# Strassen pairs for the gate and up tiles of the second group's second feed-forward

## The reference

```python
def _swiglu(x, w_gate, w_up, w_down):
    return (jax.nn.silu(x @ w_gate) * (x @ w_up)) @ w_down
x = _layer_norm(ALPHA * x + 0.5 * _swiglu(x, p['ffn2_gate'], p['ffn2_up'], p['ffn2_down']), p['ln4_g'], p['ln4_b'])
```

## Time and profile before

| | us |
|---|---|
| median of 3 runs | 2529.02 (2528.16 to 2529.35) |
| span of the profiled execution | 2523.5 |
| PE busy | 2437.7 (97%) |
| POOL busy | 1376.1 (55%) |
| ACT busy | 982.3 (39%) |
| DVE busy | 920.9 (36%) |
| the stretch from the second feed-forward of group 1 to the end | about 2105 to 2523 |

### The profile page before, as it was taken

The page is one execution under the profiler, slowest core; times in us unless marked ns, Lnnn a source line. Parts: engine busy times, 40 slices in busy tenths (PEclk is TensorE's granted clock), DMA queues, the critical chain, the costliest instruction groups (busy, mean ns, idle before and its releaser), DMA issues.

```text
span 2523.5 us, 39960 instructions
## 1 busy us (share of the span) xinstructions
PE 2437.7 (97%) x16311; PEld 2217.3 (88%) x16311; DVE 920.9 (36%) x1775; ACT 982.3 (39%) x1736; POOL 1376.1 (55%) x860
## 2 busy tenths in 40 slices
PE   8999999999999999998999999999899999999998
PEld 8888889888999999987789877888659899999998
DVE  1000002266810004277452689997264333000003
ACT  4333333534333233455543533333473435333231
POOL 4776665534666666422252676766405246666663
PEclk9999999999999999999999999999999999999999
DMA  4444532453233222533121234333402122433322
GB/s 145 123 119 117 159 94 75 139 156 104 83 94 91 86 84 79 141 107 125 45 76 35 70 102 106 110 92 100 166 1 88 48 68 81 121 109 101 92 84 69
DMA packets 425661, 245.00 MB, mean 97 GB/s; under 512 B 23008, under 2 KB 415328, under 8 KB 424720
## 3 DMA queue, kind: packets, MB, share of 16 engines
q1 hardware_dynamic: 389712, 197.88, 27.4%
q10 hardware_dynamic: 33200, 32.56, 4.0%
q0 software_dynamic: 2576, 12.07, 1.3%
HBM read 218.79 MB, written 21.74 MB: 95 GB/s over the span
## 4 chain that ended last, share of the span: by engine, by line
PE 85%; ACT 4%; DVE 4%; POOL 3%; issue 2%; DMA 1%; ACTq 0%; DVEq 0%; POOLq 0%
PE LIN L768 77%; PE TR L1109 1%; POOL WL L2093 1%; PE LIN L845 1%; PE TR L821 1%; ACT WH L1159 1%; POOL XL L2133 1%; ACT PR L1608 1%; ACT PT L1633 1%; PE LIN L1057 1%; PE TR L922 1%; DVE SC L1714 1%; PE TR L1096 1%; DVE PR L2032 1%; DVE CB L1958 1%
## 5 line engine op out<-in xcount | busy, mean ns | idle before, releaser
L2093 POOL TENSOR_TENSOR WL<-WRAW,WH 128x1024 fp32r<-128x1024 f32 (+1 forms) x378 | 889.3, 2355 | 473.9 <-ACT WH L1159 467.5
L768 PE MATMUL LIN<-XH,WH 128*128 128x256 f32 (+3 forms) x3032 | 838.2, 317 | 20.7 <-DVE Y L1782 6.5
L768 PE MATMUL LIN<-XH,WL 128*128 128x256 f32 (+3 forms) x3032 | 830.9, 315 | 0.0
L768 PE MATMUL LIN<-XL,WH 128*128 128x256 f32 (+3 forms) x3032 | 829.3, 314 | 0.0
L768 PEld LDWEIGHTS LIN<-XH,WH 128*128 128x128 f32 (+1 forms) x3032 | 529.0, 188 | 61.0 <-issue 20.0
L768 PEld LDWEIGHTS LIN<-XL,WH 128*128 128x128 f32 (+1 forms) x3032 | 528.8, 188 | 34.0
L768 PEld LDWEIGHTS LIN<-XH,WL 128*128 128x128 f32 (+1 forms) x3032 | 526.6, 188 | 33.8
L768 PE MATMUL LIN<-HH,WH 128*128 128x256 f32 (+2 forms) x1632 | 464.6, 307 | 1.7 <-POOL HL L2174 1.7
L768 PE MATMUL LIN<-HL,WH 128*128 128x256 f32 (+2 forms) x1632 | 462.1, 305 | 0.0
L768 PE MATMUL LIN<-HH,WL 128*128 128x256 f32 (+2 forms) x1632 | 461.4, 305 | 0.0
L1163 ACT ACTIVATE FG<-LIN 128x512 f32<-128x512 f32 (+3 forms) x270 | 154.9, 575 | 740.0 <-PE LIN L768 731.9
(11 more groups left out here) (200 smaller groups left out, 2048.2 us busy)
## 6 DMA issues: line engine op xcount, KB each, us to landing
WRAW<-in_ffn_gate SPq DMA_DIRECT2D x88, 512.0 KB, 3.8
WRAW<-in_ffn_up SPq DMA_DIRECT2D x88, 512.0 KB, 3.8
WRAW<-in_ffn_down SPq DMA_DIRECT2D x64, 512.0 KB, 3.8
WRAW<-in_w_mix_in SPq DMA_DIRECT2D x44, 512.0 KB, 3.8
WRAW<-in_ffn_down SPq DMA_DIRECT2D x32, 384.0 KB, 3.3
WRAW<-in_w_mix_out SPq DMA_DIRECT2D x16, 512.0 KB, 3.9
WRAW<-in_w_mem_q SPq DMA_DIRECT2D x16, 512.0 KB, 3.9
WRAW<-in_w_mem_o SPq DMA_DIRECT2D x16, 512.0 KB, 3.8
```

Source lines behind the costliest of these rows:

```text
L768: last = pe.matmul(LIN[0:pr.rows, pr.slot, out:out + w], wt[:, pr.tile % RING, c, 0:pr.rows], x[:, c, col:col + w], start=(c == 0 and wt i ...
L2093: pool.tensor_tensor(WL[:, n % RING, 0:nk, 0:width], WRAW[:, n % 2, 0:nk, 0:width], WH[:, n % RING, 0:nk, 0:width].bitcast(F32), ALU.subtr ...
```

## The change

In the second feed-forward of group 1 (`FOLDED = [(2, 1)]`) the gate tile and the up tile of a feature tile are made together as a `Pair`, except the first four tiles of part 0 and the last four of part 2: 4 + 8 + 6 = 18 pairs, 36 tiles. The two tiles are a 2×2 matrix of blocks (gate or up by first or second half of the input features), the tokens another (first or second half of the features by first or second half of the 544 columns, 272 each). Their product is made with seven half products of 4 chunks × 3 matmuls on 272 columns, after Strassen's scheme in Winograd's form, in place of eight. Four of the seven (numbers 1 to 4) have as weights a sum of blocks; numbers 0, 5 and 6 use plain blocks.

- Weight sums: DVE forms four 128x512 sums in TR (PSUM); ACT makes their high parts, DVE the low ones. The plain blocks' high parts are ACT's, the low ones POOL's. Eight half slots of WH and WL, seven used; half slot i is free when half product i of the pair before is done. A raw slot is free when all four sums (`sum_ready`) and its plain low parts (`plain_lo`) are made.
- Token sums: four blocks of 4 × 272 columns, made once from Y by DVE ("fold sums"), high parts by ACT ("fold highs"), low parts by DVE, while the four tiles in halves run. Scaling Y by ALPHA therefore moves from the norm's step 11 to the ends of the first four pairs ("scale").
- Results: four of LIN's banks hold a running chain, a sum and a single product; ACT copies the chain after half products 0 and 2 and the sum after 1; DVE adds three times; Silu is then done by ACT in FG; the last quarter is copied by ACT after half product 6.
- The strands "early" move to the down tiles 1 and 3 of parts 0 and 1.

In the diff, `...` marks what is left out.

```diff
@@ Plan.ffn
+            if folded(which, g):
+                plain = RING if split else 0
+                paired_to = len(tiles) - (RING if halves else 0)
+                ups = self.stage("ffn", g, tiles[:plain], KD, lambda k: True, which=which, after_norm=after_norm)
+                first = len(self.products) % 2
+                for k in range(plain, paired_to, 2):
+                    two = Pair(len(self.pairs), len(self.weights), g, which, part, tiles[k][1] - f0, (first + (k - plain) // 2) % 2)
...
@@ back
+            ffn[RING].mid.append(("fold sums",))
+            ffn[RING + 1].end.append(("fold highs", 0))
+            ffn[RING + 2].end.append(("fold highs", 2))
+            for k in range(KD // 2):
+                ffn[2 * RING + k].end.append(("scale", k))
@@ sync: the weight loads
-                if n >= 2:
-                    sp.wait_ge(lo_split, n - 1)
+                if n >= 2 and n - 2 in IN_PAIR:
+                    two = IN_PAIR[n - 2]
+                    sp.wait_ge(sum_ready, 4 * two.q + 4)
+                    sp.wait_ge(plain_lo, 3 * two.q + (2 if n - 2 == two.tile else 3))
+                elif n >= 2:
+                    sp.wait_ge(lo_split, COUNT[n - 2])
@@ tensor
+            def fold(two):
...
+                def half_product(i, out, hi, lo, start, fresh=None):
+                    if i in (0, 5, 6):
+                        pe.wait_ge(plain_lo, 3 * q + (1, 2, 3)[(0, 5, 6).index(i)])
+                    else:
+                        pe.wait_ge(sum_lo, 4 * q + i)
...
+                    for c in range(4):
+                        for wt, x in ((WH, hi), (WH, lo), (WL, hi)):
+                            last = pe.matmul(out, block_of(two, wt, i)[:, c, :], x[:, c, :], start=start and c == 0 and wt is WH and x is hi,
...
+                half_product(0, chain, XH[:, 0:4, 0:w], XL[:, 0:4, 0:w], True)
...
+                    pe.wait_ge(part_summed, 3 * q - 2)
+                half_product(1, summed, TH[:, 0, :, 0:w], TL[:, 0, :, 0:w], True, 0)
...
+                pe.wait_ge(part_copied, 4 * q + 1)
+                half_product(2, chain, TH[:, 1, :, 0:w], TL[:, 1, :, 0:w], False, 1)
+                pe.wait_ge(part_copied, 4 * q + 2)
+                half_product(3, summed, XH[:, 4:8, w:2 * w], XL[:, 4:8, w:2 * w], False)
+                pe.wait_ge(part_copied, 4 * q + 3)
+                half_product(4, chain, TH[:, 2, :, 0:w], TL[:, 2, :, 0:w], False, 2)
+                if not first:
+                    pe.wait_ge(part_summed, 3 * q)
+                half_product(5, single, XH[:, 4:8, 0:w], XL[:, 4:8, 0:w], True)
+                pe.wait_ge(part_summed, 3 * q + 2)
+                half_product(6, chain, TH[:, 3, :, 0:w], TL[:, 3, :, 0:w], False, 3)
@@ scalar
+            def fold(two):
...
+                act.wait_ge(part_done, 7 * q + 1)
+                if q:
+                    act.wait_ge(part_summed, 3 * q)
+                act.activation(PA[:, 0, 0:w], chain, ACT.Copy).then_inc(part_copied, 1)
+                if isinstance(two.before[0], Pair):
+                    hidden_high(two.before[0])
+                act.wait_ge(part_done, 7 * q + 2)
+                act.activation(PB[:, 0:w], sum_bank(w), ACT.Copy, scale=0.5).then_inc(part_copied, 1)
+                act.wait_ge(part_done, 7 * q + 3)
+                act.activation(PA[:, 1, 0:w], chain, ACT.Copy).then_inc(part_copied, 1)
+                for s in range(2):
+                    if on:
+                        highs_for(following, s)
+                    else:
+                        split_hi(follower(two, s), two)
+                if on:
+                    highs_for(following, 2)
+                act.wait_ge(part_summed, 3 * q + 3)
+                act.activation(FG[:, 0, 0:2 * w], FG[:, 0, 0:2 * w], ACT.Silu)
+                act.wait_ge(part_done, 7 * q + 7)
+                act.activation(FG[:, 1, 0:w], chain, ACT.Copy, scale=0.5).then_inc(part_copied, 1)
+                if on:
+                    highs_for(following, 3)
+                else:
+                    split_hi(follower(two, 2), two)
+                    hidden_high(two)
+                    split_hi(follower(two, 3), two)
@@ vector
+            def fold(two):
...
+                dve.tensor_tensor(FG[:, 0, w:2 * w], sum_bank(w), PA[:, 1, 0:w], ALU.add).then_inc(part_summed, 1)
+                if on:
+                    sum_weights(following, 1)
+                    sum_weights(following, 2)
+                dve.wait_ge(part_done, 7 * q + 5)
+                dve.scalar_tensor_tensor(FG[:, 1, w:2 * w], chain_bank(two, w), 0.5, PB[:, 0:w], ALU.mult, ALU.add)\
+                    .then_inc(part_summed, 1)
+                if on:
+                    sum_weights(following, 3)
+                    sum_weights(following, 4)
+                dve.wait_ge(part_done, 7 * q + 6)
+                dve.tensor_tensor(FG[:, 0, 0:w], single_bank(w), PA[:, 0, 0:w], ALU.add).then_inc(part_summed, 1)
+                if on:
+                    for i in (1, 2, 3, 4):
+                        sum_low(following, i)
@@ gpsimd
+            def fold(two):
+                if isinstance(two.before[0], Pair):
+                    multiply(two.before[0])
+                    plain_low(two, 6)
+                    hidden_low(two.before[0])
+                following = follower(two, 0)
+                if isinstance(following, Pair):
+                    plain_low(following, 0)
+                    plain_low(following, 5)
+                else:
+                    for s in range(3):
+                        split_lo(follower(two, s))
+                    multiply(two)
+                    hidden_low(two)
+                    split_lo(follower(two, 3))
```

More of the change, by code:

```diff
@@ L161, in tell, with __init__, folded @@
         self.kind, self.f, self.part = kind, f, part
+class Pair:
+    name, kind, pair, norm, after_norm, half, last = "ffn", "both", False, None, None, None, False
+    def __init__(self, q, tile, g, which, part, f, turn):
+        self.q, self.tile, self.g, self.which, self.part, self.f = q, tile, g, which, part, f
+        self.bank = turn
+        self.mid, self.end = [], []
+        self.event = 0
+        self.before, self.base = None, 0
+def folded(which, g):
+    return (which, g.index) in FOLDED
+FOLDED = [(2, 1)]
 class Plan:
@@ L248, in norm_strands @@
         at(3, "end", 9, 10)
-        if alpha:
+        if alpha and not folded(2, norm_stage(norm)):
             at(3, "end", 11)
@@ L342, in back @@
             for t in range(4):
-                ffn[12 + 12 * t].end.append(("early", t))
+                if folded(2, g):
+                    [pr for pr in ffn if pr.kind == "down" and pr.part == t // 2][1 + 2 * (t % 2)].end.append(("early", t))
+                else:
+                    ffn[12 + 12 * t].end.append(("early", t))
             last = [pr for pr in ffn if pr.half == 0][-4:]
@@ new lines, in highs_for, with split_next @@
+            def highs_for(two, s):
+                for i in ((0, 1), (2, 3), (4, 5), (6,))[s]:
+                    if i in (0, 5, 6):
+                        plain_high(two, i)
+                    else:
+                        sum_high(two, i)
+            def split_next(n, after):
+                following = follower(n)
+                if isinstance(following, Pair):
+                    highs_for(following, place_in(following, n))
+                elif following is not None:
+                    split_hi(following, after)
@@ L1561, in _ @@
                     before = PLAN.segments[s - 1][2][-1]
-                    split_hi(before.tile + RING, before)
+                    split_next(before.tile, before)
                     for t in range(2):
@@ L1921, in take_up @@
                     low(MEM_AT + what[0], what[0] * P, P, MH, ML)
+                elif kind == "fold sums":
+                    fold_tokens()
+                elif kind == "fold highs":
+                    fold_lows(*what)
                 elif kind == "select":
```

294 lines of the change are left out of this document (274 added, 20 removed).

## The result

The changed kernel takes 2557.43 us (median of 4 runs, 2554.77 to 2561.50), the kernel before 2528.59 beside it (2524.66 to 2529.35): ratio 1.0118, 95% interval 1.0104 to 1.0132. That is 28.8 us slower, where 15.6 were forecast; with the ratio, 29.8.

A forecast was written before the change was run, and what follows sets the result against it. TensorE, 97% busy, was the bound; with the change a 12.33 us raw-slot loop would be. Pairs −0.5 and −1.1, part ends +4.7 and +3.0, entry +6.3, +2.9 and +0.3 gave +15.6 on 2529.0: 2544.6 us, range 2530 to 2558.

The forecast's parts named there:

- the loop: Middle pairs: reloading the second raw slot waits on VectorE, ScalarE and POOL in turn, slower than PE's 10.54 us.
- The load: Weight load in each turn: lands 3.8 us after its issue; bounds worked with 3.3 and 4.1.
- the first pair of a part at 10.5: First pair of each part: finds its operands ready and takes 10.5 us.
- The half clock behind the stalls: PE's pauses: clock stays at 1.00; rival of 1.2 GHz would cost 100 us and more, chance 2%.
- The entry of part 0: First pairs of part 0: ScalarE's queue costs +6.3 us, the second raw tile's late load +2.9.
- the turn: Middle pairs, from landing to landing of the second raw tile: 12.33 us, against PE's 10.54.
- slower loads and sums in every turn (+24): Upper bound: a load at 4.1 and sums of 0.75 make 12.9 us per turn and +24 in all.
- The lower end of the sum, +3: Lower bound: a load at 3.3 and shorter POOL steps make 11.8 us per turn and about +3.
- the operation without a row: VectorE's 512-wide sum into PSUM from two SBUF inputs: 0.67 us; up to 1.98 when meeting POOL.
- Leaving a part: First down tile waits for the last hidden low part: +4.7 us in part 1, +3.0 in part 0, part 2 nothing.
- the early transposes: Four tile transposes moved to down tiles: same 0.87 us of PE, counted as nothing, up to 2 us if late.
- The shared read interface: Rival: sum 1 meets POOL's low part 0 each time, making 13.6 us per turn and 2560 in all; chance 6%.

The follow-up runs named there:

- Run 5: Changed kernel with four raw slots, odd pairs loading into two of their own: 2530.02 us, ratio 1.0006 to the kernel before.
- run 1: Changed kernel with VectorE's second fold put ahead of weight sums 1 and 2 of the next pair: 2557.02 us, ratio 1.0105 to the kernel before.
- run 4: Changed kernel with the last norm's four loads issued at the end of part 0's fourth pair: 2553.86 us, ratio 1.0098 to the kernel before.
- run 3: Changed kernel with the hidden tile finished ahead of the third down-weight split at part ends: 2548.09 us, ratio 1.0073 to the kernel before.
- run 2: Changed kernel with GpSimd making plain low part 6 before the hidden tile's multiplication: 2552.91 us, ratio 1.0090 to the kernel before.
- run 9: Changed kernel with half-size raw loads, low part 6 before the multiplication, and ScalarE's copies before the hidden high part: 2535.40 us, ratio 1.0024 to the kernel before.
- run 7: Changed kernel with the pairs' raw tiles loaded by half, 256 KB: 2539.69 us, ratio 1.0048 to the kernel before.

## Where the forecast failed, and what of it held

The mechanism held: the kernel is slower, by the loop and at the places that were named. The size did not: 28.8 us for 15.6, and 31.6 in the profiled executions, from which the shares below are taken. The steps that failed are these terms of the sum. The load was put at a constant 3.8 us, and the first pair of a part at 10.5 as if it waited for nothing: 6.3 us too little. The half clock behind the stalls was put at nothing, as a rival of all or nothing: 3.2 us at the two part ends alone. The entry of part 0 was 2.8 us too small, and the turn 0.2 us too short, 2.0 us in parts 1 and 2. Some 1.3 us of small waits behind the pairs of part 2 were not in the sum. That the result still lies near the upper end of the range is luck: that end came from slower loads and sums in every turn (+24) and from a rival, not from these terms. (The lower end of the sum, +3, isn't worked out: a turn of 11.8 in twelve pairs takes off 6.4 and leaves +9.)

- **Direction and mechanism: right.** Run 5 takes the loop away and 27 us with it; run 1 excludes the rival reading in which VectorE's order sets the pace. One place was off: in parts 1 and 2 the wait for ScalarE's copy stands before half product 3 (0.31 us, PB) and not before half product 2 (0.4 us forecast).
- **The turn, 12.33: right, 0.2 too short.** A sum takes 0.70 us, not 0.67, and overlaps less. Twelve middle pairs make 2.4 us. VectorE's sum from two SBUF inputs (L2014), the operation without a row, took 0.71 in the middle turn and 0.84 in the mean of all 18: near the lower bound.
- **The load at 3.8: right as a median, wrong as a constant.** This is the first step that failed. Three middle pairs took 13.4 to 13.9, 3.3 us over the others: their next load landed in 4.25 to 4.62 us; in two of them sum 1 then met GpSimd's low part and took 1.0; and in two the last half product ran at half clock, 0.7 and 0.3 us. The first pairs of parts 1 and 2, put at 10.5 because their operands lie ready, took 12.77 and 11.22: half product 6 waits there too for the fold behind the next pair's sums, and that pair's second tile landed late (5.49 us in part 1). The prediction had this rule for middle pairs and left it out for first ones: +3.0. With the turn (ten of its pairs lie in parts 1 and 2, 2.0 us) that makes 8.3 of the 8.4 us by which their pairs, 174.4 us, exceed the forecast 166.0. Why these loads are slow stays open: beside the one of 5.49 us nothing else was in flight, nor beside the one of 5.44 us in run 4.
- **Leaving a part: the stalls were right (4.40 us for 4.7, and 3.04 for 3.5)**, and their cause too (run 3). Missing from +4.7 and +3.0 are the half clock behind them, 1.6 us each, and the early transposes, 0.87 us each, two in either stretch. These I moved at nothing, and over the stage that is right: the gate and up tiles lost what the down tiles got.
- **Entering part 0, 6.3 + 2.9: 3 us too small.** The second load landed in 9.25 us where I took 8.2, and the first pair began 2.6 us later than forecast (36.4 us after the stage's start). Of these 2.6 us 1.1 are the half clock behind the norm's wait: in the profiled executions of runs 1 and 2, where the clock stayed up there, the first pair began after 35.2. Moving the four loads gave 3.6 us (run 4), so the +2.9 for them was fair.
- **The clock: the step that failed in its form.** I had priced it as all or nothing, 100 us at 2%, from a row in which PE was busy 1.77 of 4.00 us with the clock at 1.00. It fell seven times, for 3.4 us and once for 6.8, each time in or behind a wait of 2.1 us or more. (The Trainium skill, TensorE: Matmul & The Clock Gate, What's actually happening, says that the clock follows recent activity: the trace agrees, with 0.66 and 0.76 in the three stretches above.) Its cost here is at most 12.3 us, and 1.6 at one stall by run 3. It was a term of the sum, to be asked for at each long wait that the sum itself had found, not a rival.
- **The shared read interface:** sum 1 met POOL's low part in run 5 and took 1.14 us instead of 0.70, and 1.51 in run 9, so the effect is there. In the changed kernel the order kept the two mostly apart, as I had argued: in twelve of the 18 pairs the sum took 0.70, and the pairs were not at 13.6. (By the rule of the Trainium skill, SBUF — State Buffer, Who interferes with whom, whoever issues second is blocked until the other has finished. The traces agree: with 0.45, 0.58 and 0.95 us of GpSimd's operation to go, the sums took 1.01, 1.14 and 1.51, so each ended 0.56 us after it.)
- **Steady clock at 1.00, and 12.3 in twelve pairs,** which the text asked for: the first is refuted; of the twelve, eight are within 0.31 us of it, three are the slow landings and one, the second pair of part 0, took 11.3.

## What to carry to other kernels

Before halving the work between two loads, follow one buffer round: from its landing through every queue to the release and the next landing. If that turn is longer than the new work, saving work only makes waits, and one more buffer can be worth more than any order of instructions (27 us here, against 9 for the best reordering alone). And reordering one engine to free a buffer sooner delays what was moved back: look for who waits for that, through in-order queues, before counting the gain. A long wait that a sum foresees should be priced with and without the slower clock behind it: it counts where PE sets the pace after the wait, and not where the loop does.

## What was not expected of the hardware

- The clock came down to 1.2 GHz for 3.4 us behind some waits of 2.1 us and more and not behind others of the same length (seven of nine here; the norm's 2.2 us wait with a fall in one trace and none in another). At a part's end such a stretch cost 1.6 us (run 3); inside the loop the wait behind it shrank in turn (0.87 us before half product 6 of the fifth pair of part 1, in place of 1.45).
- A sum of 0.70 us that starts while GpSimd works on SBUF ended 0.56 us after GpSimd's operation: 1.01 us in the changed kernel, 1.14 and 1.51 in runs 5 and 9, where a reordering had brought it about.
- Two 512 KB weight loads landed 6.4 us (median) after the first was issued, whether the second was issued 2.6 or 1.3 us behind it (run 2); with 256 KB one landed in 2.9 us instead of 3.8 (run 7).
